# Moving part of a short convolution's elementwise work from VectorE to GpSimd and ScalarE

## The reference, cut to what matters

```python
def odd_layer(h, conv_prev, w_in, conv_w, w_out):
    t_ = h.shape[1]
    bg, cg, hv = jnp.split(h @ w_in, 3, axis=-1)
    z = cg * hv                                                # C * (W_in x)
    ext = jnp.concatenate([conv_prev.astype(z.dtype), z], axis=1)   # (B, CONV_BUF + T, D_CONV)
    conv = conv_w[0] * ext[:, 0:t_]
    for j in range(1, CONV_WIDTH):
        conv = conv + conv_w[j] * ext[:, j:j + t_]
    return (bg * conv) @ w_out, ext[:, -CONV_BUF:]
```

## Time and profile before

| | |
|---|---|
| median of 3 runs | 1410.09 us (1409.32 to 1548.7) |
| profiled execution | 1409.09 us |
| span of its slowest core (core 6) | 1407.5 us |
| spans of the other cores | 1402.2 to 1407.0 us |
| the stretch spoken of below as the stage | 780 to 960 us of core 6 |

### The profile page before, as it was taken

One profiled execution on the slowest core, in us unless ns is written; L12 is line 12 of the kernel. 1 busy time (PEld: TensorE's weight loads), 2 busy tenths in 40 slices (PEclk: granted clock), 3 DMA queues, 4 the chain that ended last, 5 costly groups with the idle time before them and its releaser, 6 DMA issues.

```text
span 1407.5 us, 25671 instructions; the slowest of 8 cores (1402.2 to 1407.5 us)
## 1 busy us (share of the span) xinstructions
PE 1369.1 (97%) x9153; PEld 694.3 (49%) x9153; DVE 1128.8 (80%) x2006; ACT 906.8 (64%) x1831; POOL 185.1 (13%) x265
## 2 busy tenths in 40 slices
PE   8999999999999999999999999999999999999997
PEld 4666565554454444454444444444444544444443
DVE  5896998886687778877778788999768778877778
ACT  5877878873564756863654764466747747745655
POOL 1211134343210110110100000000100100100100
PEclk9999999999999999999999999999999999999999
DMA  9672344497656864865845643630834625754613
GB/s 201 158 126 64 95 99 96 96 207 152 156 94 103 149 121 93 145 117 88 159 98 139 192 150 133 164 72 15 139 64 84 107 44 105 163 108 77 120 31 120
DMA packets 72473, 163.43 MB, mean 116 GB/s; under 512 B 6479, under 2 KB 36398, under 8 KB 72350
## 3 DMA queue, kind: packets, MB, share of 16 engines
q0 software_dynamic: 26960, 90.75, 39.4%
q1 hardware_dynamic: 45246, 70.98, 15.3%
q10 hardware_dynamic: 144, 0.07, 0.0%
HBM read 226.02 MB, written 26.55 MB: 179 GB/s over the span
## 4 chain that ended last, share of the span: by engine, by line
PE 76%; DVE 12%; ACT 6%; DMA 3%; issue 2%; DVEq 0%; POOLq 0%; ACTq 0%
PE pp L616 38%; PE pp L618 37%; ACT arena L533 3%; DMA ring<-w2w 3%; DVE mixT L568 2%; PE pp L630 2%; ACT pp L533 1%; DVE arena L568 1%; DVE x_sb L568 1%; DVE hT L568 1%; DVE arena L586 1%; DVE arena L1864 1%; DVE x_sb L574 1%; DVE x_sb L586 1%; DVE ring L568 1%
## 5 line engine op out<-in xcount | busy, mean ns | idle before, releaser
L533 ACT ACTIVATE pp<-pp 128x512 f32<-128x512 f32 x456 | 260.0, 582 | 287.4 <-PE pp L616 194.5
L568 DVE TENSOR_TENSOR x_sb<-x_sb,pp 128x512 f32<-128x512 f32 (+1 forms) x392 | 293.0, 774 | 94.0 <-ACT pp L533 41.7
L618 PE MATMUL pp<-hT,ring 128*128 128x512 f16 (+2 forms) x1468 | 252.3, 309 | 1.6 <-ACT arena L533 1.0
L533 ACT ACTIVATE arena<-arena 128x512 f16<-128x512 f16 (+1 forms) x285 | 173.9, 625 | 27.3 <-DVE arena L1864 18.0
L618 PEld LDWEIGHTS pp<-hT,ring 128*128 128x128 f16 x1468 | 109.6, 97 | 106.9 <-issue 4.0
L616 PE MATMUL pp<-hT,ring 128*128 128x512 f16 x648 | 160.1, 379 | 2.2 <-ACT pp L533 2.0
L533 ACT ACTIVATE arena<-pp 128x512 f32<-128x512 f32 (+2 forms) x224 | 131.0, 588 | 47.9 <-PE pp L618 27.1
L616 PE MATMUL pp<-ring,arena 128*128 128x512 f16 x512 | 130.5, 379 | 0.8 <-ACT pp L533 0.8
L616 PEld LDWEIGHTS pp<-hT,ring 128*128 128x128 f16 x648 | 62.2, 98 | 78.2 <-issue 6.5
L618 PE MATMUL pp<-ring,mixT 128*128 128x512 f16 x416 | 96.8, 379 | 1.3 <-DVE mixT L568 1.2
L616 PE MATMUL pp<-mixT,arena 128*128 128x512 f16 x368 | 92.6, 379 | 0.0
(11 more groups left out here) (266 smaller groups left out, 2317.3 us busy)
## 6 DMA issues: line engine op xcount, KB each, us to landing
ring<-w2w POOLq DMA_DIRECT2D x50, 512.0 KB, 9.1
ring<-w1w POOLq DMA_DIRECT2D x45, 512.0 KB, 9.4
ring<-wsc SPq DMA_DIRECT2D x24, 896.0 KB, 5.5
ring<-wst POOLq DMA_DIRECT2D x41, 512.0 KB, 8.7
x_sb<-xp SPq DMA_DIRECT2D x28, 512.0 KB, 6.0
extra<-w1w POOLq DMA_DIRECT2D x15, 512.0 KB, 8.1
yp<-x_sb SPq DMA_DIRECT2D x14, 512.0 KB, 3.0
x_sb<-st_hgrn SPq DMA_DIRECT2D x24, 256.0 KB, 4.3
```

The costliest lines, as they stand in the source:

```text
L533: return e.activation(out=out, in_=in_, func=func, bias=bias, scale=scale)
L568: return Op(eng, lambda e: e.tensor_tensor(out=out, in0=in0, in1=in1, op=op), R, W, *span(0.066, 0.15, n, two))
L618: ins = e.matmul(o, l, r, start=s, stop=t)
```

## The change

It does three things. The second half of the value product, `G * B`, is issued on POOL instead of DVE. The third tap is no longer one DVE operation: ACT scales the shifted `Z` by `w2` in place, and POOL adds the result to `D`. And the two gate products whose gate lies in SBUF are issued on POOL; the two with the gate in PSUM stay on DVE.

```diff
                 if what == "22":
-                    yield TT(G, G, B, ALU.mult, BG + BB, BG)
+                    yield TT(G, G, B, ALU.mult, BG + BB, BG, eng="pool")
                     flags.add(T("z1"))
...
                     yield STT(D, Z[:, 1:1025], w1, D, ALU.mult, ALU.add, BZ + BG + BD + [B_small], BD)
-                    yield STT(D, Z[:, 2:1026], w2, D, ALU.mult, ALU.add, BZ + BG + BD + [B_small], BD)
+                    yield ACT(Z[:, 2:1026], Z[:, 2:1026], AF.Copy, BZ + BG + [B_small], BZ + BG, scale=w2)
+                    yield TT(D, D, Z[:, 2:1026], ALU.add, BZ + BG + BD, BD, eng="pool")
...
                 yield TT(mixT[:, 2 * i + j, tokslice(t0 + r)], src, D[:, 512 * r:512 * (r + 1)], ALU.mult, Bs + BD,
-                         [B_mix[2 * i + j][t0 + r]])
+                         [B_mix[2 * i + j][t0 + r]], eng="dve" if k is not None else "pool")
```

## The result

The change makes the kernel slower: 1420.57 us as the median of its runs (1419.53 to 1420.77), 1409.76 for the kernel before beside it (1409.32 to 1410.09). The ratio is 1.0075, 95% interval 1.0052 to 1.0098; by the medians the loss is 10.8 us. By the bound of two per cent that is no change; by its interval it is a loss. The forecast was 1412, a loss of 3.

What follows compares the result with a forecast made beforehand. PE was taken to bound the stage (busy 172.86 of 180 us), DVE close behind. Gain -2.5 and loss +5.5 (path 3.0, one hold 2.5) gave +3.0 on 1409.09: 1412 us, range 1404 to 1425.

Steps and rivals of the forecast that it cites:

- a longer path: From a value unit's last block out of PSUM to finished `D`: 7.4 instead of 4.4 us, 3.0 lost, counted once.
- holds: DVE operations with two SBUF inputs stand still while POOL computes: 20 us on DVE in the stage, bounds 0 and 81.3.
- a gain at the end: PE's two waits for DVE at the stage's end, 1.8 and 0.7 us, go: 2.5 us gained.
- the forecast's own band: Time of the whole kernel if the main forecast holds, 1408 to 1417 us, chance 0.50.
- queue rival: POOL's in-order queue: products wait behind loads, ACT's scalings and PE's copies behind them; 1418 to 1430 us, chance 0.15.
- exclusion rival: Every POOL instruction holds DVE for its whole length; DVE needs 196 us in the 180 us stage: 1425 us, chance 0.07.
- loads: Busy time in the stage of 180 us: DVE 135 (130 to 140), ACT 124, POOL 86 us.
- my bound from two products: POOL's add of 1024 elements taken as two 512-element products, 2.54 us.
- one unplanned hold by a POOL add on top, 2.5 us: One hold in the stage by a POOL add, 2.5 us, added to the path's 3.0 for 5.5 us lost.
- a slip, once made: PE's slip against planned order covers the same lateness of all later units, so path loss counts once, not 16 times.
- Relief: DVE at 135 instead of 157 us in the stage evacuates earlier, hiding the longer path: 1402 to 1407 us, chance 0.20.
- Z rival: Only two Z buffers, freed 3.0 us later, stop PE in every unit: 48 us more, 1457 us, chance 0.08.

Runs made afterwards that it cites:

- run 9: Changed kernel, same order, POOL's 48 convolution instructions made MEMSETs as long as those replaced (no SBUF reads, arithmetic left out): 1408.28 us, ratio 0.9991.
- run 1: Changed kernel, same order, POOL's 48 convolution instructions made MEMSETs shorter than those replaced (no SBUF reads, arithmetic left out): 1405.50 us, ratio 0.9962.
- Run 3: Kernel before with only the gate products from SBUF moved to POOL, taps and z products left as they were: 1414.64 us, ratio 1.0025.

## Why the prediction was right and wrong

The direction and the range held. The mechanism held in part: a longer path, holds and a gain at the end all stood in the sum, but the holds, its smaller loss, are all of the measured one. The point was 8.6 us low, and the forecast's own band (1408 to 1417) missed. The time lies in the band of the queue rival (1418 to 1430), which is not what made it, and the range reached it only by the price of the exclusion rival, in a form that did not come: that the range held is partly luck. By its steps:

- **The loads held.** DVE was to be at 130 to 140 us and is at 140.0, ACT at 124 and is at 123.5, POOL at 86 and is at 80.6 (780 to 970 us, since the stage ends some 8 us later; in 780 to 960 they are 130.0, 115.3 and 79.7). PE's idle time, foretold as near 10 us, is 14.4. The addition takes 2.18 us, not 2.54; the estimate from the Trainium skill's GPSIMD Engine Reference (section 3.1), 2.25, was nearer than my bound from two products.
- **The total of the holds held, at 16.8 us for my 20.** The changed kernel and run 9 have the same 1958 DVE instructions in the same order; the page gives 1113.8 and 1097.0 us busy. The holds of copies, some 4 us, are in both and not in this number. What fell differently is on whom, and how: I looked for some 23 holds (52 x 0.45) of 0.85 us, spread over all instructions, the scaled adds too (1.6 us expected, 1.35 measured); there were 14, of 1.1 us on the mean, and five of the short sums, which follow each other in DVE's queue, had 6.6 of the 15.5 us.
- **What failed is the term "one unplanned hold by a POOL add on top, 2.5 us".** By the changed kernel and run 9, the holds cost 12.3 us of time. The premise was that a slip, once made, covers the lateness of later units, as long as the loads have room. The runs show that one slip does not cover the next: the holds at 800, 908 and 955 us each cost PE anew, and taking away the eight instructions there gives 7.9 us back. DVE is free for 50 of the stage's 190 us, but its queue is in order; the evacuation behind the four held sums at 798.68 came some 4 us late, and PE waited 2.52 for it.
- **The path and the gain nearly held together.** Without the holds the change is worth -1.3 us (run 9, interval -2.8 to +0.1); I had +0.5 (3.0 for the path, less 2.5 for the waits at the end). The waits for DVE at the stage's end did go, as counted, in run 9; in the changed kernel another one of 2.7 us, for `extra`, stands there.
- **The rivals.** Relief is what the change would bring if POOL did not read and were faster: run 1 stands 4.0 us below before, run 9, at full length, only 1.3. The exclusion rival (1425) was right in kind and wrong in its condition: it was to decide when holds fill DVE's whole stage, 65 us of them, and 16.8, some in bad places, were enough. The queue rival was a part: the wait at 908 us is made of POOL's order, and 2.1 of its 3.0 us stay without holds; but it was not a load or a DMA that made it, as I had thought. The Z rival did not come: PE has four waits over 1 us in the stage, not one in every unit.
- **The rule of the Trainium skill** ("SBUF — State Buffer", Who interferes with whom), that a DVE instruction with two SBUF inputs and a POOL instruction that reads SBUF exclude each other, and one that only writes does not, is borne out on both sides by these runs. With POOL's reads the short sums take 599 and 840 ns, beside writes alone 285. POOL waits for DVE in its turn (2.02 us for a product of 1.29). I had used it for DVE's load and not for the order of what stands behind.

## What to carry to other kernels

In this kernel work moved to POOL beside a DVE that does two-input work cost by what stands behind the held instruction in DVE's queue, not by the sum of the holds: look for evacuations behind small SBUF sums, and price each such place apart. Whether it is the holds or the longer path is told by a kernel in which POOL writes for as long but reads nothing, in the same order. And a part that gives 1 us of loss by one plan gave 6 by another, so a single re-planned order says little about the edit.

## What the runs showed of the hardware that was not expected

A DVE copy with one SBUF input is held too, even by POOL's writes: the copies `arena<-gsm` of two columns took 596 ns on the mean beside MEMSETs (run 9) and 161 in the kernel before, while the two-input sums beside the same MEMSETs were not held (285 ns). The row of the kernel before, 780 to 960 us:

```profile
L592 DVE COPY arena<-gsm 128x2 f32<-128x2 f32 x8 | 1.2, 161 | 0.0
```

In run 9 one of them began at 900.06 us, 0.35 us into a MEMSET, and ended 0.03 us after it. The same section of the Trainium skill's "SBUF — State Buffer" has copies in a two-port mode among what contends; whether a copy of two columns runs in such a mode no run here shows. The prediction had counted only instructions with two inputs.

A long wait of PE can cost twice. In the stage of the kernel before the granted clock is 1.00; after the wait of 3.05 us that ends at 911.16 the stretch from 910 to 915 us has 0.66, a stretch at the lower of the two levels, 1.2 instead of 2.4 GHz, for a part of it. By 0.34 of 5 us that is an estimated 1.7 us of PE's time. It does not follow every such wait. On this core the stretches behind the waits of 2.5 and 2.7 us keep 1.00; all eight cores have the same three waits to 0.1 us, and the clock fell behind the one of 3.05 us on five of them. On core 2 it fell behind none; its stretches around the end of that wait, at 908.20:

```profile
905.00:910.00 5.00, 1.95 (x9) 0.71 (x8) 5.00 (x8) 2.73 (x4) 1.38 (x1) 1.00 0.38 145
910.00:915.00 5.00, 4.59 (x23) 2.20 (x23) 4.97 (x6) 2.39 (x5) 2.48 (x1) 1.00 0.00 0
```

What decides it no run here shows. Nor does it explain what the holds cost: on the slowest core of run 9 the clock falls as far after its wait of 2.1 us (0.83 from 900 to 910 us, in the changed kernel 0.83 from 910 to 920). Run 3 shows a fall after its wait of 5.4 us:

```profile
860.00:865.00 5.00, 1.34 (x4) 0.55 (x5) 4.61 (x5) 0.00 (x0) 1.17 (x1) 0.74 0.25 106
865.00:870.00 5.00, 5.00 (x15) 1.85 (x14) 0.00 (x0) 2.27 (x4) 0.00 (x0) 0.58 0.00 0
```

PE is busy for all of the second stretch, at a granted clock of 0.58. No term of the prediction stood for that.
